# Cross attention behind a recurrence: operands fetched in the recurrence's last head, splits dealt over the first step, the next rows split in the last step

## What is computed

```python
m = rms_norm(mem, mem_norm_w[layer])                     # 256 memory rows
mk, mv = jnp.split(jnp.einsum('bmd,de->bme', m, w_mem_kv[layer]), 2, axis=-1)
s = jnp.einsum('bhsd,bhmd->bhsm', split_heads(xq, 4), split_heads(mk, 4)) * (128 ** -0.5)
p = jax.nn.softmax(s, axis=-1)
xo = jnp.einsum('bhsm,bhmd->bhsd', p, split_heads(mv, 4))
xo = merge_heads(rms_norm(xo, xattn_norm_w[layer]))
...
mixed = jnp.concatenate([gla_o, hgrn_o, xo], axis=-1)    # 1024 + 512 + 512 rows
mixed = mixed * jax.nn.silu(gate)
x = x + jnp.einsum('bse,ed->bsd', mixed, w_out[layer])
```

## Time and profile before

| | |
|---|---|
| time, median of 3 runs | 2489.32 us (2489.11 to 2491.13) |
| the profiled execution's own time | 2497.34 us |
| its span in the trace | 2495.5 us |
| PE busy | 2377.8 us, 95% of the span |
| DVE, ACT, POOL busy | 1291.0, 911.1, 780.4 us |
| bytes moved | 314.01 MB |
| mean granted TensorE clock | 0.979 of full speed |

### The profile page before, as it was taken

The page is one execution under the profiler, slowest core; times in us unless marked ns, Lnnn a source line. Parts: engine busy times, 40 slices in busy tenths (PEclk is TensorE's granted clock), DMA queues, the critical chain, the costliest instruction groups (busy, mean ns, idle before and its releaser), DMA issues.

```text
span 2495.5 us, 38973 instructions
## 1 busy us (share of the span) xinstructions
PE 2377.8 (95%) x15376; PEld 2054.2 (82%) x15376; DVE 1291.0 (52%) x2607; ACT 911.1 (37%) x1677; POOL 780.4 (31%) x711
## 2 busy tenths in 40 slices
PE   6999989999999598989999999999999999999995
PEld 5778978888878598989888889777898777787795
DVE  3001349999998333154232454455455455577535
ACT  4214554444433334033222233333333344554321
POOL 3111315545543022132334332333233232231123
PEclk9999999999999799999999999999999999999998
DMA  4333344343323432222233443234224324465611
GB/s 188 126 111 122 133 149 147 120 140 116 122 94 124 173 135 68 76 115 84 100 126 102 146 136 113 93 121 142 86 94 147 106 73 174 156 240 201 216 51 68
DMA packets 139767, 314.01 MB, mean 126 GB/s; under 512 B 12352, under 2 KB 56000, under 8 KB 128336
## 3 DMA queue, kind: packets, MB, share of 16 engines
q1 hardware_dynamic: 80624, 224.67, 26.3%
q10 hardware_dynamic: 58976, 87.05, 9.7%
HBM read 212.58 MB, written 99.09 MB: 125 GB/s over the span
## 4 chain that ended last, share of the span: by engine, by line
PE 83%; DVE 8%; DMA 3%; issue 2%; ACT 2%; POOL 1%; SPq 0%; POOLq 0%; DVEq 0%; ACTq 0%
PE bank L408 11%; PE bank L410 11%; PE bank L409 11%; PE bank L419 9%; PE bank L420 8%; PE bank L421 8%; PE bank L2360 3%; PE bank L2338 3%; PE bank L1723 3%; PE bank L1721 3%; PE bank L1722 3%; PE bank L1398 1%; PE bank L2327 1%; PE bank L690 1%; PE bank L2645 1%
## 5 line engine op out<-in xcount | busy, mean ns | idle before, releaser
L408 PE MATMUL bank<-at_hi,w_hi 128*128 128x512 f32 x1408 | 584.8, 415 | 6.6 <-ACT stage L444 4.2
L419 PE MATMUL bank<-w_hi,at_hi 128*128 128x256 f32 x1920 | 558.8, 291 | 7.6 <-DVE at_lo L1598 6.8
L410 PE MATMUL bank<-at_hi,w_lo 128*128 128x512 f32 x1408 | 554.4, 394 | 0.0
L409 PE MATMUL bank<-at_lo,w_hi 128*128 128x512 f32 x1408 | 552.9, 393 | 0.0
L420 PE MATMUL bank<-w_lo,at_hi 128*128 128x256 f32 x1920 | 545.8, 284 | 0.0
L421 PE MATMUL bank<-w_hi,at_lo 128*128 128x256 f32 x1920 | 545.6, 284 | 0.0
L374 POOL TENSOR_TENSOR w_lo<-w_raw,w_hi 128x2048 fp32r<-128x2048 f32 x69 | 318.1, 4611 | 649.8 <-ACT w_hi L387 625.7
L419 PEld LDWEIGHTS bank<-w_hi,at_hi 128*128 128x128 f32 x1920 | 371.6, 194 | 20.6 <-issue 11.4
L420 PEld LDWEIGHTS bank<-w_lo,at_hi 128*128 128x128 f32 x1920 | 371.1, 193 | 0.8 <-issue 0.2
L421 PEld LDWEIGHTS bank<-w_hi,at_lo 128*128 128x128 f32 x1920 | 370.6, 193 | 0.0
L408 PEld LDWEIGHTS bank<-at_hi,w_hi 128*128 128x128 f32 x1408 | 270.2, 192 | 79.7 <-issue 22.5
(11 more groups left out here) (296 smaller groups left out, 3615.0 us busy)
## 6 DMA issues: line engine op xcount, KB each, us to landing
w_raw<-in_weights SPq DMA_DIRECT2D x84, 1024.0 KB, 7.7
feat<-stage ACTq DMA_DIRECT2D x184, 256.0 KB, 2.0
tok<-stage ACTq DMA_DIRECT2D x72, 256.0 KB, 2.2
stage<-feat SPq DMA_DIRECT2D x32, 256.0 KB, 3.5
x<-in_x SPq DMA_DIRECT2D x4, 1024.0 KB, 9.6
w_mem<-in_w_mem SPq DMA_DIRECT2D x4, 1024.0 KB, 11.6
logg<-gate_g ACTq DMA_DIRECT2D x8, 512.0 KB, 2.9
rec_b<-logg SPq DMA_DIRECT2D x16, 256.0 KB, 5.2
```

Of the source, the lines that this page charges most:

```text
L408: nc.tensor.matmul(ps_gemm[i % 2], wh, ah, start=(k == 0), stop=False)
L409: nc.tensor.matmul(ps_gemm[i % 2], wh, al, start=False, stop=False)
L410: last = nc.tensor.matmul(ps_gemm[i % 2], wl, ah, start=False, stop=(k == KT - 1))
L419: nc.tensor.matmul(o, ah, wh, start=(k == 0), stop=False)
```

## The change

Stage 3's first loads move into the last head of stage 2 and are issued as their memory comes free; load 3 is also split there, and the first step's scores are put before the last transpose of the recurrence. In stage 3 loads 4 to 7 are split between the first step's own instructions, and the last weight block of the recurrence is split there too, its low part on POOL and no longer on DVE. The second fill is loaded during stage 3; its token half 0 is split in the last step (load 3 and 7 of it are taken from `cmx` in place and no longer go through DRAM), half 1 right behind stage 3. Stage 3's loop is written out, and `con` and `cjunk` share memory with `cp` and `cpT`. Its core:

```diff
@@ head_sp, last head
             if not after:
                 sp.wait_ge(r_st, 16 * (2 * HEADS + 1))
                 fill_load(sp, mix_slots, mixT[0:D, :], FILLED0, range(3))
+                sp.wait_ge(gate_silu, 2 * 2 * HEADS)
+                fill_load(sp, mix_slots, mixT[0:D, :], FILLED0, range(3, 4))
+                sp.wait_ge(r_o, head * 8 + (6 + 8))
+                sp.dma_start(cmk[:].rearrange("p h m -> p (h m)"), mk_dram).then_inc(c_mem, 16)
+                block_stored(sp, REC_BLOCKS - 3)
+                cross_queries(sp, 0)
+                sp.wait_ge(r_R, head * 8 + (8 + 1))
+                sp.dma_start(X[:, :, 0:HALF], I["x"].rearrange("(t p) d -> p t d", p=P)[:, :, 0:HALF]).then_inc(x_in, 16)
+                sp.wait_ge(r_o, head * 8 + (8 + 8))
+                sp.dma_start(cmv[:].rearrange("p t n -> p (t n)"), mv_dram).then_inc(c_values, 16)
+                block_stored(sp, REC_BLOCKS - 2)
+                cross_gates(sp, 0)
+                fill_load(sp, mix_slots, mixT[0:D, :], FILLED0, range(4, 7))
             sp.wait_ge(r_mx, head * 8 + (8 + 1))
@@ head_pe_rec
+            if not after:
+                cross_scores(pe, 0, 0, 0)
             rec_turn(pe, head, mixer, NT - 1)
@@ p3_sp
+            fill_load(sp, mix_slots, mixT[0:D, :], FILLED0, range(7, LOADS))
+            cross_queries(sp, 1)
+            cross_gates(sp, 1)
             beside_cross.weights(sp, 0)
...
+            for j in range(2):
+                sp.wait_ge(c_st[j], 16 * 2)
+            for n in (0, 1, 2, 4, 5, 6):
+                rest_load(sp, n)
@@ new in stage 3
+        REST_SLOTS = {0: 0, 1: 1, 2: 2, 4: 3, 5: 0, 6: 1}
+        def rest_load(sp, n):
+            slot, h, rows = REST_SLOTS[n], n // 4, D + n % 4 * (2 * P)
+            if n > 4:
+                sp.wait_ge(fill_lo, FILLED1 + 2 * slot + 2)
+            sp.dma_start(rest_slots[slot], mixT[rows:rows + 2 * P, half(h)].rearrange("(a p) n -> p a n", p=P)
+                         ).then_inc(part_in[slot], 16)
+        def rest_high(act, loads):
+            for n in loads:
+                if n % 4 == 3:
+                    act.wait_ge(c_mx, 4 + 2 * PAIRS + 3 + n // 4)
+                else:
+                    act.wait_ge(part_in[REST_SLOTS[n]], 16 * (5 if n > 4 else 4))
+                for a in range(2):
+                    nc.scalar.activation(at_hi[:, n % 4 * 2 + a, half(n // 4)], rest_slice(n, a), ACT.Copy).then_inc(fill_hi, 1)
@@ p3_act
-            fill_high(act, mix_slots, 0, range(3, 4))
             all_products(act, gemm_rec)
-            split_high(act, *rec_block(REC_BLOCKS - 1))
-            fill_high(act, mix_slots, 0, range(4, LOADS))
-            with act.Fori(0, PAIRS) as it:
+            fill_high(act, mix_slots, 0, range(4, 5))
+            for it in range(PAIRS):
...
+                    if last:
+                        act.wait_ge(tile_done, 4 * (gemm_out[0][0].first + 3) + 10)
+                        rest_high(act, range(4))
                     act.wait_ge(c_nm, it * 4 + (n + 1))
...
+                    if first:
+                        fill_high(act, mix_slots, 0, range(5, 6))
+                        split_high(act, *rec_block(REC_BLOCKS - 1))
                     beside_cross.results(act, it, 4 * n + 1)
                     act.wait_ge(c_t, it * 4 + (n + 1))
@@ p3_dve
-            fill_low(dve, mix_slots, FILLED0, range(3, 4))
-            low_after(dve, REC_BLOCKS * 4 - 1)
-            fill_low(dve, mix_slots, FILLED0, range(4, LOADS))
...
+                    if last:
+                        rest_low(dve, range(2))
                     beside_cross.sums(dve, it, 4 * n + 1)
@@ p4_act
             all_products(act, gemm_out[0])
-            fill_high(act, rest_slots, 1, range(LOADS))
+            rest_high(act, range(4, LOADS))
+            beside_cross.results(act, PAIRS - 1, 15)
```

More of the change, by code:

```diff
@@ L179, in build @@
                 cpT = sb("ca_pT", [P, CH, MT, P], F32, part)
-                con = sb("ca_on", [P, CH, P], F32, part)
-                cjunk = sb("ca_junk", [P, CH, P], F32, part)
+                con = cp[:, 0:2, :].rearrange("p a (b n) -> p (a b) n", n=P)
+                cjunk = cpT[:, :, 0, :]
                 cmx = sb("ca_mx", [P, 2, TOK], F32, part)
@@ L1316, in head_act_rec @@
                     fill_high(act, mix_slots, 0, range(3))
+            if not after:
+                fill_high(act, mix_slots, 0, range(3, 4))
             normed(act, head, mixer, NT - 1)
@@ new lines, in rest_high, with rest_low @@
+        def rest_high(act, loads):
[6 more added lines that the diff above has]
+                    nc.scalar.activation(at_hi[:, n % 4 * 2 + a, half(n // 4)], rest_slice(n, a), ACT.Copy).then_inc(fill_hi, 1)
+        def rest_low(dve, loads):
+            for n in loads:
+                for a in range(2):
+                    k, here = n % 4 * 2 + a, half(n // 4)
+                    dve.wait_ge(fill_hi, FILLED1 + 2 * n + a + 1)
+                    nc.vector.tensor_tensor(at_lo[:, k, here], rest_slice(n, a), at_hi[:, k, here].bitcast(F32),
+                                            ALU.subtract).then_inc(fill_lo, 1)
@@ new lines, in cross_scores @@
+        def cross_scores(pe, it, j, hf):
+            n = 2 * j + hf
+            if n == 0 and it == 0:
+                pe.wait_ge(c_mem, 16)
+            if hf == 0:
+                pe.wait_ge(c_in[j], it * 16 + 16)
+            pe.wait_ge(c_e, it * 16 + (4 * n + 4))
+            for b in range(CH):
+                t = CH * hf + b
+                last = nc.tensor.matmul(ps_a[:, b // 2, (b % 2) * MEM:(b % 2 + 1) * MEM], cq[:, j, t * P:(t + 1) * P],
+                                        cmk[:, it * 2 + j, :], start=True, stop=True)
+            last.then_inc(c_s, 1)
@@ L1517, in p3_act @@
                                              scale=small[:, 16 + b:17 + b], accum_out=small[:, 20 + b:21 + b]).then_inc(c_ss, 1)
-                    beside_cross.results(act, it, 4 * n + 3)
-                    if hf == 1:
+                    if first:
+                        fill_high(act, mix_slots, 0, range(7, LOADS))
+                    if not last:
+                        beside_cross.results(act, it, 4 * n + 3)
+                    if hf == 1 and it < PAIRS - 1:
                         act.wait_ge(c_mx, it * 4 + (n + 5))
-                        act.dma_start(mixT[3 * 512:4 * 512, :][bass.ds(it * (2 * P) + j * P, P), :], cmx[:, j, :]).then_inc(c_st[j], 16)
-            for j in range(2):
-                act.wait_ge(c_st[j], 16 * (PAIRS + 1))
+                        head = it * 2 + j
+                        act.dma_start(mixT[3 * 512 + head * P:3 * 512 + (head + 1) * P, :], cmx[:, j, :]).then_inc(c_st[j], 16)
         def p3_pool(pool):
-            with pool.Fori(0, PAIRS) as it:
+            for it in range(PAIRS):
                 for j, hf, n in halves():
+                    if n == 0 and it == 0:
+                        low_after(pool, REC_BLOCKS * 4 - 1)
                     for i in range(3):
@@ L1534, in p3_dve @@
         def p3_dve(dve):
-            fill_low(dve, mix_slots, FILLED0, range(3, 4))
-            low_after(dve, REC_BLOCKS * 4 - 1)
-            fill_low(dve, mix_slots, FILLED0, range(4, LOADS))
-            with dve.Fori(0, PAIRS) as it:
+            for it in range(PAIRS):
                 for j, hf, n in halves():
-                    if n == 0:
-                        dve.wait_ge(x_in, it * 16 + 16)
+                    first, last = it == 0 and n == 0, it == PAIRS - 1 and n == 3
+                    if n == 0 and it:
+                        dve.wait_ge(x_in, 16 * 2)
                     beside_cross.sums(dve, it, 4 * n)
@@ L1552, in p3_dve @@
                     nc.vector.tensor_scalar(small[:, 16:20], small[:, 12:16], P ** -0.5, None, ALU.mult).then_inc(c_r, 1)
+                    if first:
+                        fill_low(dve, mix_slots, FILLED0, range(5, 7))
+                    if last:
+                        rest_low(dve, range(2, 4))
                     beside_cross.sums(dve, it, 4 * n + 2)
```

79 lines of the change are left out of this document (37 added, 42 removed).

## The result

The changed kernel takes **2455.24 us** (median of 4 runs, 2453.76 to 2459.75); the kernel before took 2490.23 us beside it (4 runs, 2489.11 to 2492.13). The ratio is 0.9859, with a 95% interval of 0.9843 to 0.9875. The prediction was 2456 us.

A forecast was written before the change was run, and what follows sets the result against it. PE, busy 95% of the span, bounds the kernel; only its idle time and slow clock can be won. Gains of 23.8 + 9.2 = 33.0 us take 2497.34 to 2464.3 us, the median 8.02 lower: 2456.3 us, range 2450 to 2465.

The forecast's parts named there:

- The early loads, load 3 and the scores cost nothing: Recurrence's last head: early loads, load 3's split and the scores add no wait; stage 3's first part starts at about 819.7.
- Ceiling 30.0 us: Start of stage 3: gain up to the second step's scores if nothing waits, 30.0 us.
- First wait 3.4 us: First step: PE waits 3.4 us for the exponentials, which stand behind load 4's high part in ACT's stream.
- Second wait 1.7 us: First step: PE waits 1.7 us for the copy `cpT`, behind load 5 and the weight block on ACT.
- Clock 1.0 us: First step: PE's clock may or may not fall in the 3.4 us wait; 1.0 us taken, 2.4 us if tripped.
- The sign "another wait of 1 to 2 us before the first product": Changed trace, first step: PE would wait 1 to 2 us before the first product with the values.
- Third, a tie of 0.1 us: First step: DVE's `con` is ready after 6.0 us, PE's work takes 5.9 us; 0.1 us lost.
- DVE pays for POOL's port, POOL does not: First step, weight block's low part on POOL: DVE's low parts wait, POOL is not late; otherwise 1.3 us lost.
- Part 1, 23.8 us: Start of stage 3: gain after the waits and the clock's loss, 23.8 us, bounds 19.8 to 27.0.
- Part 2, 9.2 us: End of stage 3: the 6.8 us wait before `gemm_out[1]` and 2.4 us of half clock go; lower bound 6.8.
- Part 3, nothing: The rest, including stage 3's written-out loop: no gain, since clean steps show no wait for register rows.
- The step from the profiled execution to the median, 8.02 us: Whole kernel: median taken 8.02 us below the profiled execution, turning 2464.3 us into 2456.3 us.

The follow-up runs named there:

- experiment 9: Changed kernel with the first step's splits ordered by when PE needs them, loads 4 and 5 behind the copy, weight block's low part on DVE: 2451.41 us.
- experiment 1: Changed kernel with the end of stage 3 undone: second fill loaded and split in stage 4, last two heads' rows through DRAM again: 2469.16 us.
- experiment 7: Changed kernel with the low part of the recurrence's last weight block on DVE, not on POOL: 2456.07 us, ratio 0.9867.
- 10: Changed kernel and that of experiment 9, both unaltered, rerun in one sitting: 2456.95 us and 2451.76 us.
- experiment 6: Changed kernel with ACT's split of the last recurrence weight block moved behind the copy of the transposed probabilities in the first step: 2457.45 us, ratio 0.987.

## Why the prediction was right

Point by point, with what each was predicted to be:

- **The early loads, load 3 and the scores cost nothing**: so it is. The scores lie around the last transpose, and the first part starts at 811.64, on the old axis 819.96 (predicted 819.7).
- **Ceiling 30.0 us**: 29.7, and 23.21 of it came. A step without waits takes 16.26 us from its first part in experiment 9 (predicted 16.2), so its end is at 827.90, or 836.2 on the old axis.
- **First wait 3.4 us**: 3.9. Load 4 landed 1.0 us later than I took it; PE came to the wait 0.5 us later too.
- **Second wait 1.7 us**: 0. **Clock 1.0 us**: 2.6. These two terms were mis-sized, and by the same mechanism: the clock did fall, and a slower PE came to the copy when it was ready. The prediction names that overlap (the second wait hides a part of the clock's loss), but priced it from the other side. Their sum was 2.7 and measured 2.6. That it fits so well is partly luck: 1.0 was a value between a fall and none, and in the traces of experiments 1, 7 and 10, whose first step is the same or nearly so, the clock took 2.1, 2.5 and 2.2 us beyond the waits, since it fell at other moments. The sign "another wait of 1 to 2 us before the first product" did not come.
- **Third, a tie of 0.1 us**: no wait. Experiment 6 shows how near: POOL's split 2.2 us later made PE wait 1.7 us there.
- **DVE pays for POOL's port, POOL does not**: 3.44 us against 1.29 on DVE, 4.56 on POOL, and nothing on the path (0.14 us in experiment 7). Where the split runs later, in experiment 6, POOL's root took 0.8 us longer (2.07 against 1.31) beside DVE's low parts, so this holds for that place and not in general. The Trainium skill (GPSIMD Engine Reference, Specifications) says that the two contend for SBUF where DVE's instruction has two inputs there; the trace agrees, and shows the contention to be without a price at this place.
- **Part 1, 23.8 us**: 23.21. **Part 2, 9.2 us**: 9.50, with the last transposes followed at once by the next tile. **Part 3, nothing**: 0.35 us over seven steps, and 0.9991 [0.9981, 1.0] for the loop alone. The sum of 33.06 meets the 33.0 more closely than its parts do, since their misses cancel.
- **The step from the profiled execution to the median, 8.02 us**: its cause was not known then. The prediction let the changed kernel's profiled execution carry the same 8 us (2464.3 us); it took 2455.30. The traces show half speed in three stretches of the recurrence, which the kernel before had in that execution and the changed one had not.
- **The Trainium skill's advice against gaps between bursts** (TensorE: Matmul & The Clock Gate, Why this matters for your kernels): the prediction said that the trace had no gap as short as the one foretold. It overlooked two of 2.3 and 2.6 us, some 100 us behind the region, each with half speed behind it:

```profile
1083.37 3.58 PE L702 MATMUL bank<-ident,X 128*128 128x128 f32 x16 [2.27 <-DVE at_lo L1645]
1109.08 2.90 PE L702 MATMUL bank<-ident,X 128*128 128x128 f32 x16 [2.64 <-DVE at_lo L1645]
1083.00:1087.00 4.00, 3.63 (x18) 3.63 (x19) 3.63 (x7) 2.86 (x7) 0.01 (x1) 0.57 0.00 0
1110.00:1114.00 4.00, 4.00 (x23) 3.67 (x21) 3.92 (x7) 2.65 (x5) 0.00 (x0) 0.58 1.03 416
```

Read then, they would have spoken for a fall. The changed kernel's gap is 3.9 us, and the clock fell in it; so it did in all eight executions with a wait of 2.6 to 4.9 us in the first step.

## What to carry to other kernels

When a prefetch is moved earlier, look at what stands behind its consumer in that engine's stream: a split placed by the order of arrival held up exponentials that needed nothing of it, and moving only the exponentials sent the same wait one instruction further. Ask of every split when the matrix engine reads its result, and place it just ahead of that. Before blaming the order of transfers, try that of the instructions: two moves of X only put the wait elsewhere, and dealing the splits by need gave 6.5 us in the trace (3.8 and 5.2 in the medians). And line two traces up by the same instruction ahead of the change before subtracting: here 8.3 of 41.4 us had nothing to do with it.

## What the runs showed of the hardware

- A store of 256 KB, issued by SP right behind a transfer of 2 MB and three of 512 KB, took SP 5.05 us to issue in place of 0.33, and in the second execution of the changed kernel two weight blocks took 14.26 us to issue. An issue behind a backlog can hold the issuing engine, and all that waits for it.
- Between 818 and 826 us the transfers moved 390 to 430 GB/s with a share of 1.04 to 1.07; a share of 1.01 went with 345 GB/s in the earlier trace rows. A share near 1 is therefore no fixed rate.
- PE's clock fell to 1.2 GHz some 2.7 us into a wait of 3.9 us, and that cost 2.6 us more. The moment varies: in the other executions it fell from 2.2 us into the first step's wait to 0.8 us after a wait of 4.0 us had ended (experiment 1). In experiment 9, without a wait, it didn't fall. A wait of 3.9 to 4.9 us has cost 1.4 to 1.7 times its length in this step.
- Shorter waits can cost as well: at the two waits of 2.3 and 2.6 us at line 702, which every variant has, the clock fell in 16 of 22 cases in eleven executions. In the second execution of the changed kernel it fell at neither.
